# Expert weights with two neighbouring rows to a partition, columns reordered by the copies, and the third scatter tile on four quarters

## What is computed

```
logits = u @ router_w + router_b                # 320 rows, 32 experts, top 4, softmax over the four
hcat   = xblk @ w_up[e] + b_up[e]               # 1024 -> 2048
x_glu, x_lin = hcat[:, :1024], hcat[:, 1024:]
x_glu  = min(x_glu, 7);  x_lin = clip(x_lin, -7, 7)
a      = x_glu * sigmoid(1.702 * x_glu) * (x_lin + 1)
y      = a @ w_down[e] + b_down[e]              # 1024 -> 1024
out[row] += gate * y
x      = LN2(alpha * x + (1 + gate2) * out)
```

## Time and profile before

| | us |
|---|---|
| median of 3 runs | 1505.88 (1501.29 to 1507.79) |
| profiled execution | 1502.87 |
| its span | 1501.1 |
| TensorE matmul busy | 1415.1 (94%) |
| VectorE busy | 499.0 (33%) |
| ScalarE busy | 244.7 (16%) |
| hardware DMA queue of SP | 86.1% of 16 engines |

### The profile page before, as it was taken

The page is one execution under the profiler, slowest core; times in us unless marked ns, Lnnn a source line. Parts: engine busy times, 40 slices in busy tenths (PEclk is TensorE's granted clock), DMA queues, the critical chain, the costliest instruction groups (busy, mean ns, idle before and its releaser), DMA issues.

```text
span 1501.1 us, 22079 instructions
## 1 busy us (share of the span) xinstructions
PE 1415.1 (94%) x7645; PEld 578.4 (39%) x7646; DVE 499.0 (33%) x1127; ACT 244.7 (16%) x431; POOL 13.7 (1%) x22
## 2 busy tenths in 40 slices
PE   5999999999949999999999999999999999999993
PEld 2654666665533333333333323333333333333331
DVE  2210355554671223232323232323222332313336
ACT  0001334442020111111111111111111111101110
POOL 0000000000010000000000000000000000000000
PEclk9999999999969999999999999999999999999997
DMA  9948456999857789999999988999999999998941
GB/s 337 391 167 315 176 185 266 419 424 386 251 192 278 284 352 401 418 418 418 415 418 417 419 352 359 406 418 418 417 416 419 417 418 416 418 401 322 385 191 35
DMA packets 95716, 523.72 MB, mean 349 GB/s; under 512 B 10172, under 2 KB 10485, under 8 KB 55498
## 3 DMA queue, kind: packets, MB, share of 16 engines
q1 hardware_dynamic: 92512, 517.62, 86.1%
q0 software_dynamic: 1344, 4.90, 0.8%
q10 hardware_dynamic: 1834, 0.84, 0.3%
HBM read 519.87 MB, written 3.46 MB: 349 GB/s over the span
## 4 chain that ended last, share of the span: by engine, by line
PE 83%; DMA 8%; DVE 5%; SPq 2%; issue 2%; ACT 0%; DVEq 0%
PE ps L1635 28%; PE ps L1713 14%; PE ps L1578 7%; PE ps L1192 6%; PE ps L1252 5%; PE ps L1556 5%; DMA arena<-in_cache_v 4%; PE ps L1480 3%; DMA arena<-in_w_in 2%; PE ps L1627 2%; PE ps L1249 2%; PE ps L1422 2%; DMA arena<-in_w_up 2%; PE ps L1645 1%; PE ps L1405 1%
## 5 line engine op out<-in xcount | busy, mean ns | idle before, releaser
L1635 PE MATMUL ps<-arena 128*64 128x512 f32 x2048 | 451.9, 599 | 0.6 <-DMA arena<-in_w_up 0.6
L1635 PEld LDWEIGHTS ps<-arena 128*64 128x64 f32 x2048 | 144.7, 138 | 306.7 <-issue 304.2
L1713 PE MATMUL ps<-arena 128*64 128x512 f32 x1024 | 226.8, 595 | 0.0
L1094 DVE TENSOR_TENSOR arena<-arena,ps 128x512 f32<-128x512 f32 (+1 forms) x198 | 124.4, 680 | 220.6 <-PE ps L1578 214.9
L1192 PE MATMUL ps<-arena 128*128 128x128 f32 (+4 forms) x1075 | 151.6, 282 | 33.6 <-DVEq L975 10.9
L1138 DVE TENSOR_SCALAR arena<-ps 128x512 f32<-128x512 f32 (+1 forms) x35 | 24.2, 692 | 419.7 <-PE ps L1635 358.6
L1192 PEld LDWEIGHTS ps<-arena 128*128 128x128 f32 (+4 forms) x1075 | 116.8, 144 | 107.9 <-issue 80.3
L1713 PEld LDWEIGHTS ps<-arena 128*64 128x64 f32 x1024 | 70.7, 137 | 152.2 <-issue 152.2
L1578 PE MATMUL ps<-arena 64*128 64x512 f32 x444 | 122.1, 635 | 4.9 <-DVE arena L1118 4.6
L1556 PE MATMUL ps<-arena 128*64 128x512 f32 (+1 forms) x396 | 97.1, 608 | 2.3 <-DVE arena L1082 2.3
L670 ACT ACTIVATE arena<-arena 128x512 f32<-128x512 f32 (+1 forms) x35 | 22.1, 632 | 447.8 <-DVE arena L1138 447.8
(11 more groups left out here) (225 smaller groups left out, 839.7 us busy)
## 6 DMA issues: line engine op xcount, KB each, us to landing
arena<-in_w_up SPq DMA_DIRECT2D x256, 1024.0 KB, 14.4
arena<-in_w_down SPq DMA_DIRECT2D x128, 1024.0 KB, 12.4
arena<-in_w_ada SPq DMA_DIRECT2D x12, 2048.0 KB, 17.8
arena<-in_cache_k SPq DMA_DIRECT2D x16, 1536.0 KB, 14.3
arena<-in_cache_v SPq DMA_DIRECT2D x16, 1536.0 KB, 9.7
arena<-in_w_in SPq DMA_DIRECT2D x6, 2048.0 KB, 20.5
arena<-in_cache_k SPq DMA_DIRECT2D x32, 192.0 KB, 12.9
arena<-in_cache_v SPq DMA_DIRECT2D x32, 192.0 KB, 10.9
```

The lines of the kernel that those rows point to most:

```text
L1094: ins = v_.tensor_tensor(acc[0:n, tt, 512 * h:512 * h + 512], acc[0:n, tt, 512 * h:512 * h + 512], bank(banks[h])[0:n], ALU.add)
L1635: ins = mm(bank(part)[64 * h:64 * h + 64], xe_t[:, 0, at:at + 64], up_w[:, k, FF * part + 512 * h:FF * part + 512 * h + 512], start=False, ...
L1713: ins = mm(bank(3)[64 * h:64 * h + 64], a_t[:, 0, at:at + 64], dn_w[:, kk, 512 * h:512 * h + 512], start=kk == 0, stop=kk == KC - 1)
```

## The change

Four things are done together.

1. Layout. `(k p) n` becomes `(m p k) n` for the up weights and `(m k p) n` becomes `(m p k) n` for the down weights: partition p gets the features 256 m + 2 p and 256 m + 2 p + 1, which are neighbours in HBM. A DMA of `up_w` now carries two chunks (2 MiB, one run of 16 KB to a partition), and there are four of them with four semaphores; a DMA of `dn_w` carries the same 1 MiB as before in runs of 8 KB. SP waits for the second chunk of the pair (`2 * m + 2`), TensorE waits once for each pair.
2. Reordering. So that the other operand has the same feature order, ScalarE's copy of the gathered rows reads PSUM with a step of two and writes packed, and VectorE's last product reads packed and writes with a step of 128 between neighbours, now into `act_g` instead of `act_l`.
3. The third tile. `scatter_sample` takes each of the two row halves and two column quarters as its own matmul, 64 x 64 by 256 columns; the sample rows' columns 0 to 255 of a half lie on partitions 0 to 63 and columns 256 to 511 on partitions 64 to 127 of the bank. `add_back` for this tile is one instruction over 128 partitions, and `finish` reads `acc` in four parts. The last scatter does the same, the down bias included.
4. The wait of `add_last` for `sc_added` moves ahead of the branch.

```diff
--- before.py
+++ after.py
@@ -240,8 +240,8 @@
         wada_d = t["w_ada"][0].rearrange("(k p) n -> p k n", p=128)
         win_d = t["w_in"][0].rearrange("(k p) n -> p k n", p=128)
         wo_d = t["w_o"][0].rearrange("(k p) n -> p k n", p=128)
-        wup_d = t["w_up"][0].rearrange("e (k p) n -> e k p n", p=128)
-        wdn_d = t["w_down"][0].rearrange("e (m k p) n -> e m p k n", p=128, k=2)
+        wup_d = t["w_up"][0].rearrange("e (m p k) n -> e m p k n", p=128, k=2)
+        wdn_d = t["w_down"][0].rearrange("e (m p k) n -> e m p k n", p=128, k=2)
         ck = t["cache_k"][0].rearrange("b s h e -> b s (h e)")
         cv = t["cache_v"][0].rearrange("b s h e -> b s (h e)")
 
@@ -251,7 +251,7 @@
         ada_used, ada_late, hot_in, k_high_in, v_in, wo_in = map(
             sem, ("ada_used", "ada_late", "hot_in", "k_high_in", "v_in", "wo_in"))
         k_low_in = [sem(f"k_low_in{half}") for half in range(2)]
-        up_in = [sem(f"up_in{k}") for k in range(KC)]
+        up_in = [sem(f"up_in{m}") for m in range(KC // 2)]
         dn_in = [sem(f"dn_in{m}") for m in range(KC // 2)]
         bup_in, bup_used, up_used, dn_used = map(sem, ("bup_in", "bup_used", "up_used", "dn_used"))
         const_in, c_in, rows_in, bada_in, bada_late, x_ready, tabc_in = map(
@@ -439,14 +439,14 @@
             sp.dma_start(x1[:, 1, :], t["x_prompt"][0, 128:256, :]).then_inc(x_late, 16)
             sp.dma_start(x1[0:64, 2, :], t["x_sample"].rearrange("b s d -> (b s) d")).then_inc(x_late, 16)
             sp.wait_ge(v_used, NB)
-            for k in range(4):
-                sp.dma_start(up_w[:, k, :], wup_d[0, k]).then_inc(up_in[k], 16)
+            for m in range(2):
+                sp.dma_start(up_w[:, 2 * m:2 * m + 2, :], wup_d[0, m]).then_inc(up_in[m], 16)
             sp.wait_ge(so_copied, NB)
             for b in range(NB):
                 src = vectors[1 + b:2 + b, 0:3 * D].to_broadcast([NS, 3 * D]).rearrange("p (a b) -> p a b", a=3)
                 sp.dma_start(mod_s[NS * b:NS * b + NS], src).then_inc(mod_late, 16)
-            for k in range(4, KC):
-                sp.dma_start(up_w[:, k, :], wup_d[0, k]).then_inc(up_in[k], 16)
+            for m in range(2, KC // 2):
+                sp.dma_start(up_w[:, 2 * m:2 * m + 2, :], wup_d[0, m]).then_inc(up_in[m], 16)
             for m in range(KC // 2):
                 if m == 1:
                     sp.wait_ge(u2_ready, 3)
@@ -457,10 +457,10 @@
             with sp.Fori(1, items) as i:
                 e = i % NE
                 load_expert(e, i)
-                for k in range(KC):
-                    sp.wait_ge(up_used, (i - 1) * KC + k + 1)
-                    sp.dma_start(up_w[:, k, :], wup_d[bass.ds(e, 1), k].rearrange("o p n -> (o p) n")
-                                 ).then_inc(up_in[k], 16)
+                for m in range(KC // 2):
+                    sp.wait_ge(up_used, (i - 1) * KC + 2 * m + 2)
+                    sp.dma_start(up_w[:, 2 * m:2 * m + 2, :], wup_d[bass.ds(e, 1), m].rearrange(
+                        "o p k n -> (o p) k n")).then_inc(up_in[m], 16)
                 for m in range(KC // 2):
                     sp.wait_ge(dn_used, (i - 1) * (KC // 2) + m + 1)
                     sp.dma_start(dn_w[:, 2 * m:2 * m + 2, :], wdn_d[bass.ds(e, 1), m].rearrange(
@@ -654,7 +654,8 @@
                 act.wait_ge(ga_done, turn_no)
                 for v in reversed(range(blocks)):
                     w = 256 if v else 512
-                    ins = nc.scalar.copy(xe_nat[:, v, 0:w], bank(4 + v, 0, w))
+                    ins = nc.scalar.copy(xe_nat[:, v, 0:w].rearrange("p (m k q) -> p m k q", k=2, q=128),
+                                         bank(4 + v, 0, w).rearrange("p (m q k) -> p m k q", k=2, q=128))
                 ins.then_inc(xn_ready, 1)
 
             gathered(2, 1)
@@ -1089,6 +1090,10 @@
                 return ins
 
             def add_back(tt, banks):
+                if tt == 2:
+                    rows = acc[:, 2, 0:512].rearrange("p (h n) -> p h n", h=2)
+                    both = ps[:, 512 * banks[0]:512 * banks[0] + 1024].rearrange("p (h n) -> p h n", h=2)
+                    return v_.tensor_tensor(rows, rows, both[:, :, 0:256], ALU.add)
                 n = TILES[tt][1]
                 for h in range(2):
                     ins = v_.tensor_tensor(acc[0:n, tt, 512 * h:512 * h + 512], acc[0:n, tt, 512 * h:512 * h + 512],
@@ -1139,7 +1144,9 @@
                     V(v_.tensor_scalar(l, lin, 7.0, -7.0, ALU.min, ALU.max))
                     V(v_.scalar_tensor_tensor(l, l, 1.0, g, ALU.add, ALU.mult))
                     dve.wait_ge(sig_ready[v], i + 1)
-                    v_.tensor_tensor(l, l, sg, ALU.mult).then_inc(a_ready[v], 1)
+                    v_.tensor_tensor(g.rearrange("p (m k q) -> p m q k", k=2, q=128),
+                                     l.rearrange("p (m q k) -> p m q k", k=2, q=128),
+                                     sg.rearrange("p (m q k) -> p m q k", k=2, q=128), ALU.mult).then_inc(a_ready[v], 1)
 
                 dve.wait_ge(up_used, i * KC + KC)
                 swiglu(0)
@@ -1169,7 +1176,16 @@
                 dve.wait_ge(sc_added, items * 3 + 2 + tt)
                 dve.wait_ge(g2_done, tt + 1)
                 at = 512 * (0, 6, 4)[tt]
-                V(v_.scalar_tensor_tensor(fin_t[0:n], ps[0:n, at:at + 1024], 1.0, acc[0:n, tt, :], ALU.add, ALU.mult))
+                if tt < 2:
+                    ins = v_.scalar_tensor_tensor(fin_t[0:n], ps[0:n, at:at + 1024], 1.0, acc[0:n, tt, :], ALU.add, ALU.mult)
+                else:
+                    for part in range(2):
+                        for h in range(2):
+                            z = 512 * h + 256 * part
+                            ins = v_.scalar_tensor_tensor(fin_t[0:n, z:z + 256], ps[0:n, at + z:at + z + 256], 1.0,
+                                                          acc[64 * part:64 * part + 64, 2, 256 * h:256 * h + 256],
+                                                          ALU.add, ALU.mult)
+                V(ins)
                 V(v_.scalar_tensor_tensor(fin_t[0:n], x1[0:n, tt, :], ALPHA, fin_t[0:n], ALU.mult, ALU.add))
                 norm_sums(V, v_, fin_t[0:n], n, st, var_ready)
                 norm_rows(dve, V, v_, fin_t[0:n], n, st, ln2, sd_ready, 6 + tt, fin_y[0:n, tt, :])
@@ -1571,6 +1587,16 @@
                         ins = turn(bank(1 + 2 * v, 128 * c, 128 * c + 128), xe_nat[:, v, 128 * c:128 * c + 128], 128)
                 ins.then_inc(gathered_turned_done, 1)
 
+            def scatter_sample(banks, blocks, more=False):
+
+                for v in range(blocks):
+                    for part in range(2):
+                        for h in range(2):
+                            ins = mm(bank(banks[h], 0, 256)[64 * part:64 * part + 64], sel_t[64 * h:64 * h + 64, v, 256:320],
+                                     y_sb[64 * h:64 * h + 64, v, 256 * part:256 * part + 256],
+                                     start=v == 0, stop=v == blocks - 1 and not more)
+                return ins
+
             def scatter(tt, banks, blocks, more=False):
 
                 for v in range(blocks):
@@ -1581,13 +1607,20 @@
 
             def last_scatter(blocks):
 
-                for tt, banks in enumerate(((6, 7), (4, 5), (2, 3))):
+                for tt, banks in enumerate(((6, 7), (4, 5))):
                     a, n = TILES[tt]
                     scatter(tt, banks, blocks, more=True)
                     for h in range(2):
                         ins = mm(bank(banks[h])[0:n], gt_sb[0:NE, a:a + n], bd_sb[0:NE, 512 * h:512 * h + 512],
                                  start=False, stop=True)
                     ins.then_inc(sc_done, 1)
+                scatter_sample((2, 3), blocks, more=True)
+                for part in range(2):
+                    for h in range(2):
+                        at = 512 * h + 256 * part
+                        ins = mm(bank(2 + h, 0, 256)[64 * part:64 * part + 64], gt_sb[0:NE, SEQ:NTOK],
+                                 bd_sb[0:NE, at:at + 256], start=False, stop=True)
+                ins.then_inc(sc_done, 1)
 
             def gate2(tt, b):
 
@@ -1655,7 +1688,8 @@
                     ins.then_inc(bup_used, 1)
                     for k4 in range(0, KC, 4):
                         for k in range(k4, k4 + 4):
-                            pe.wait_ge(up_in[k], i * 16 + 16)
+                            if k % 2 == 0:
+                                pe.wait_ge(up_in[k // 2], i * 16 + 16)
                             ins = up_main(k)
                             if blocks == 1:
                                 ins.then_inc(up_used, 1)
@@ -1678,7 +1712,7 @@
                 def turn_act(v):
                     p = 64 if v else 128
                     for c in range(4):
-                        ins = turn(bank(2 * v, p * c, p * c + p), act_l[0:p, v, 128 * c:128 * c + 128], p)
```

(5 more changed lines are left out.)

## The result

The changed kernel takes 1517.32 us (median of 7 runs, 1511.23 to 1520.77); the kernel before, beside it on the same chip, 1501.29 us (7 runs, 1500.29 to 1507.79). The ratio is 1.0093, with an interval of 1.0075 to 1.0110: it is slower, where 13 us of gain were forecast. One run, of the kernel before with late loads, took 1810.26 us at a granted clock of 0.77 and is left out of that ratio. The profiled execution after took 1520.77 us with a span of 1519.0, against 1502.87 and 1501.1. So there are 17.9 us of span to explain.

The account below looks back on a forecast made before the run. TensorE was taken to set the time, with DMA 5% behind. Scatter -14.8, product +2.4, stall -0.8 and tail -0.2 sum to -13.4 us, giving 1492.5 us; range 1486 to 1498, chance 60%.

Parts of the forecast that it names:

- the place of the saving: Third scatter tile on TensorE: all 14.8 us saved counts as time gained, bounds 1.8 and 19.
- the moved wait: Wait for `sc_added`, moved ahead of the branch: asks for an add finished long before, so costs 0.
- A: DMA queues not relieved by the longer rows; slowest engine stays at 30.9 us, stalls return; 1501.5 us, chance 15%.
- B: Scatter on array quarters saves nothing, eight small matmuls costing as much as four wide; 1505.5 us, chance 9%.
- C: Pairs of 16 KB rows run worse, so DMA becomes the bound; at 2% worse 1516 us, chance 9%.
- D: VectorE's scattered product write is much dearer, so turns wait in every item; 1514 us at 2.0 us each, chance 7%.
- The scatter: Sample tile's scatter on TensorE: 1.06 us becomes 0.65; with two blocks 0.82 us is saved from 1.92.
- The turn: One single-block pass of the expert loop on TensorE: 29.41 us becomes 29.0.
- The product: VectorE's last activation product, written with a step: 0.69 becomes about 1.09 us; hidden except in three second-block items, +2.4 us.
- ScalarE's strided read: ScalarE's copy of gathered rows, reading every second float of PSUM: costs 0; +2.6 us kept for the range.
- The weights: Weight DMAs with half the packets: mean engine 30.2 to 29.6 us an item, slowest engine 29.9 to 30.3.
- the old stall of 0.8 us: TensorE's wait for up weights near 1309 us: goes, none replaces it, -0.8 us; bound of +1 for a new one.

Follow-up runs that it names:

- the kernel before with late loads: Kernel before, with two of TensorE's three flag loads moved from the loop's head to behind up; 1500.82 us, ratio 0.9977.
- the run with halves: Kernel before, third scatter cut into twice as many matmuls of 256 columns over the same tiles; 1514.32 us, ratio 1.0085.
- The kernel with two loads more: Kernel before, with two more flag loads, values unused, at the head of TensorE's loop; 1515.16 us, ratio 1.0084.
- the kernel with late loads: Changed kernel, with two of TensorE's three flag loads moved from the loop's head to behind up; 1493.78 us, ratio 0.9928.
- the quarters alone: Kernel before with only the third scatter tile on four array quarters and its shared add; old weights, copies and product; 1516.06 us, ratio 1.0082.

## Why the prediction was wrong

**The step that failed** is the place of the saving: "All of it is on the path, as the scatter stands between down and the turned choice with no gap at either side". There was no gap because the scatter covered something, and I read the absence of a gap as the absence of anything behind it. What was missing from the sum is a term, the sequencer's way round the loop, of 3.5 us or more. It had its row: the bias line's idle time before, four gaps and 5.7 us "<-issue", three of them 0.7 us long behind the second-block items. I asked what the scatter's VectorE add and the moved wait would cost, not what its four matmuls hid. That the moved wait costs nothing held, by the run with halves. In the four double turns and the three second-block ones the scatter's saving came back whole as a gap, and in the double ones 1.4 us more than that. The forecast of 1492.5 us also started 4.6 us high, from a median of three runs (1505.88) that seven put at 1501.29.

**The clock was taken as fixed.** No step of mine said so, because no term had it; it is the largest one, 22 us where 18 were lost in all. A gap of 2.3 us costs itself and then 1.7 or 3.4 us, for a half-clock stretch of 3.4 or 6.8; the gaps of 1.2 us had such a stretch behind them too. The kernel with two loads more shows it without any edit to the scatter.

**Rivals.** None of the four was it: A, B, C and D all put the mishap in DMA, the array or VectorE; none put it in the sequencer. That the measured time stands next to C's 1516 is chance: DMA ran at 426 GB/s.

**Right, by their steps.** The scatter: 0.65 us forecast, 0.60 measured; double 1.10, and 1.02. The turn: 29.0, and 28.95. The product: 1.09 us, and 1.06 (median of 35, below), not awaited in single-block items, and 3 x 2 x 0.40 = 2.4 us in the others, where 1.9 came (5.6 - 3.7). ScalarE's strided read cost nothing that shows. The line's answer, min/median/max in ns:

```profile
L1147 DVE TENSOR_TENSOR arena<-arena x35: 1036/1061/1093, 470.6 to 1472.0; 128x512 f32<-128x512 f32 x32, 64x512 f32<-64x512 f32 x3
```

That a write which steps from line to line is dearer, as the Trainium skill has it in "SBUF — State Buffer", note on cachelines, was borne out, and its price is near the one that the earlier trace rows gave for another step (0.78): 1.06 - 0.69 = 0.37 us for 512 elements, 0.72 ns each.

The weights: from 600 to 840 us 9348 packets for 102.19 MB at 426 GB/s, against 17793 and 417.

```profile
DMA packets 9348, 102.19 MB, mean 426 GB/s; under 512 B 1055, under 2 KB 1055, under 8 KB 1055
```

With 1055 small ones taken off, 8293 data packets for 8.1 items of 1024: a row of 16 KB is one packet. The mean engine needs 12.60/0.426 = 29.6 us, as worked out.

**One term mis-sized.** I had the old stall of 0.8 us gone and none in its place. The landing times of the up loads grow by 1.3 to 1.4 us a turn, just above the 0.9 to 1.3 forecast (issues from 1046 and 1278 us, eight turns apart: (24.0 - 13.2)/8 = 1.35):

```profile
DMA to landing us min/median/max: 11.0/13.2/15.4
...
DMA to landing us min/median/max: 21.8/24.0/26.3
```

So, by inference, the slowest engine needs 28.95 + 1.35 = 30.3 us, the upper of my two values: it stays 0.7 above the mean, and not by packets. Turns that wait for weights bear both values out. They follow each other at 30.35 us in the kernel with late loads, which has the new rows, and at 1320.80 - 1289.91 = 30.89 us with the quarters alone, which have the old rows. The former:

```profile
1276.77 3.65 PE L1666 MATMUL ps<-arena 128*64 128x512 f32 x16 [1.12 <-DMA arena<-in_w_up]
...
1307.12 3.65 PE L1666 MATMUL ps<-arena 128*64 128x512 f32 x16 [1.18 <-DMA arena<-in_w_up]
```

In the changed kernel the slack was spent by the last turn of the long run:

```profile
1305.93 10.52 PE L1668 MATMUL ps<-arena 128*64 128x512 f32 x48
1317.48 3.65 PE L1668 MATMUL ps<-arena 128*64 128x512 f32 x16 [1.03 <-DMA arena<-in_w_up]
1320.97 1.46 PE L1572 MATMUL ps<-arena 128*64 128x512 f32 x6
```

Up took 1320.97 - 1305.93 = 15.04 us, 1.3 over its 13.78; the bound of +1 that I gave a new stall was a little short. At this size it decided nothing.

## What to carry to other kernels

Where a matmul stream crosses the turn of a loop, list what the sequencer has to do there (branches, loads of registers, waits) and what is queued ahead of it, by its time and by its count; short matmuls were poor cover here, and an edit that makes them more and shorter has to be paid for by moving loads away from the turn. A line whose idle time is ended by "issue" in a few turns is a warning that time saved ahead of it will not be gained there; how much cover the other turns have is found by adding loads. Price a new gap on TensorE with the clock behind it, which here cost about as much again or more.

## What the runs showed of the hardware

- A register load of a flag in TensorE's sequencer takes 0.64 to 0.67 us (two added: a gap from 0.73 to 2.01, from 0.69 to 2.03) or 0.78 us (two removed: from 2.28 to 0.72). Behind up, such loads opened no gap.
- What covers the sequencer is not time alone: 16 matmuls of 256 columns that take as long as 8 of 512 left a gap of 1.34 us where there was none. A fixed number of instructions does not explain all of it.
- Behind gaps of 0.7 to 2.3 us at the turn the granted clock fell to half for 3.4 or 6.8 us, in some turns and not in others: in the kernel before behind two of three gaps of 0.7 us, in the changed one behind all seven of 1.2 to 2.3.
- The slowest DMA engine, inferred from landing times and from the pace of turns that wait, stays 0.7 us an item behind the mean: 30.9 against 30.2 us with 2048 packets an item, 30.3 against 29.6 with 1024.
- A transpose that reads every second column of its input takes 1.15/8 = 0.144 us instead of 0.128.
